# Router logits of a mixture-of-experts kernel in plain f32, with two weight splits moved ahead of the routing

## What is computed

```
def moe_swiglu(x, router_w, router_b, w_gate_up, w_down):
    B, S, D = x.shape                      # 1, 256, 1024
    xf = x.reshape(-1, D)
    logits = jnp.einsum('td,de->te', xf, router_w) + router_b     # 8 experts
    top_v, top_i = lax.top_k(logits, TOP_K)                       # TOP_K = 2
    gates = jax.nn.softmax(top_v, axis=-1)
    combine = jnp.sum(gates[..., None] * jax.nn.one_hot(top_i, N_EXPERTS), axis=1)
    for e in range(N_EXPERTS):
        y = y + combine[:, e:e + 1] * swiglu(xf, w_gate_up[e], w_down[e])
```

## Time and profile before

| what | us |
|---|---|
| median of 3 executions | 2058.91 |
| lowest and highest | 2049.66, 2062.65 |
| the profiled execution, its own time | 2062.65 |
| its span | 2060.9 |
| mean granted TensorE clock, share of full | 0.954 |

### The profile page before, as it was taken

How to read it: one execution, slowest core, us unless ns; L and a number is a source line. 1 busy time by engine, 2 the same in 40 slices (tenths; PEclk the granted TensorE clock), 3 DMA queues, 4 the chain that set the end, 5 groups by cost and what they waited for, 6 DMA issues and landing times.

```text
span 2060.9 us, 26596 instructions
## 1 busy us (share of the span) xinstructions
PE 1961.6 (95%) x10038; PEld 1608.1 (78%) x10051; DVE 1395.9 (68%) x1162; ACT 1129.9 (55%) x991; POOL 59.2 (3%) x81
## 2 busy tenths in 40 slices
PE   8978999999999998798999999999999999999987
PEld 6756998786789976686778778778787877888875
DVE  4444776444454545537888878888788888888875
ACT  5333554352243433514666767767676676776762
POOL 2230000100000000000000000000000000000000
PEclk8979999998899999778999999999999999999999
DMA  6604445442245545113999989999999999999980
GB/s 232 203 31 143 160 166 184 154 143 82 82 149 203 193 134 184 62 42 104 359 333 325 360 315 346 349 326 355 333 349 347 321 345 326 345 356 329 351 296 31
DMA packets 251591, 486.93 MB, mean 236 GB/s; under 512 B 14108, under 2 KB 19292, under 8 KB 251536
## 3 DMA queue, kind: packets, MB, share of 16 engines
q1 hardware_dynamic: 244976, 477.30, 65.9%
q0 software_dynamic: 6560, 8.91, 1.5%
HBM read 484.05 MB, written 1.05 MB: 235 GB/s over the span
## 4 chain that ended last, share of the span: by engine, by line
PE 59%; DMA 14%; DVE 13%; ACT 7%; issue 4%; DVEq 2%; SPq 0%; POOL 0%; ACTq 0%; POOLq 0%
DMA w_raw<-in_moe_w_down 8%; DVE w_lo L887 7%; PE psum L1908 7%; PE psum L1910 7%; PE psum L1909 7%; PE psum L1500 6%; PE psum L1502 6%; PE psum L1501 6%; ACT w_hi L521 6%; DMA w_raw<-in_moe_w_gate_up 6%; PE psum L1531 3%; PE psum L1533 3%; PE psum L1534 3%; PE psum L1551 2%; PE psum L1654 1%
## 5 line engine op out<-in xcount | busy, mean ns | idle before, releaser
L887 DVE TENSOR_TENSOR w_lo<-w_raw,w_hi 128x2048 fp32r<-128x2048 f32 (+2 forms) x475 | 1029.7, 2196 | 354.5 <-ACT w_hi L521 351.0
L521 ACT ACTIVATE w_hi<-w_raw 128x2048 fp32r<-128x2048 f32 (+2 forms) x475 | 862.3, 1838 | 273.4 <-DMA w_raw<-in_moe_w_gate_up 105.7
L1908 PE MATMUL psum<-w_hi,xg_hi 128*128 128x512 f32 x896 | 361.0, 403 | 0.8 <-DVE xg_lo L1333 0.4
L1909 PE MATMUL psum<-w_lo,xg_hi 128*128 128x512 f32 x896 | 355.1, 396 | 0.0
L1910 PE MATMUL psum<-w_hi,xg_lo 128*128 128x512 f32 x896 | 355.0, 396 | 0.0
L1531 PE MATMUL psum<-xt_hi,w_hi 128*128 128x256 f32 (+1 forms) x840 | 235.2, 280 | 2.5 <-DVE w_lo L887 1.9
L1533 PE MATMUL psum<-xt_lo,w_hi 128*128 128x256 f32 (+1 forms) x840 | 234.7, 279 | 0.0
L1534 PE MATMUL psum<-xt_hi,w_lo 128*128 128x256 f32 (+1 forms) x840 | 234.5, 279 | 0.0
L1908 PEld LDWEIGHTS psum<-w_hi,xg_hi 128*128 128x128 f32 x896 | 169.0, 189 | 41.4 <-DVE w_lo L887 2.5
L1910 PEld LDWEIGHTS psum<-w_hi,xg_lo 128*128 128x128 f32 x896 | 168.9, 189 | 41.0
L1909 PEld LDWEIGHTS psum<-w_lo,xg_hi 128*128 128x128 f32 x896 | 169.2, 189 | 37.9
(11 more groups left out here) (362 smaller groups left out, 2041.6 us busy)
## 6 DMA issues: line engine op xcount, KB each, us to landing
w_raw<-in_moe_w_gate_up SPq DMA_DIRECT2D x224, 1024.0 KB, 6.7
w_raw<-in_moe_w_down SPq DMA_DIRECT2D x96, 1024.0 KB, 7.0
w_raw<-in_w_up SPq DMA_DIRECT2D x22, 1024.0 KB, 5.6
w_raw<-in_ffn_w_gate_up SPq DMA_DIRECT2D x22, 1024.0 KB, 5.5
w_raw<-in_moe_w_down SPq DMA_DIRECT2D x32, 512.0 KB, 4.5
w_raw<-in_w_in SPq DMA_DIRECT2D x12, 1024.0 KB, 6.7
w_raw<-in_ab_w_in SPq DMA_DIRECT2D x12, 1024.0 KB, 5.2
w_raw<-in_w_down SPq DMA_DIRECT2D x10, 1024.0 KB, 6.3
```

Source lines behind the costliest of these rows:

```text
L521: return act.activation(o, i, func, **kw)
L887: TT(w_lo[:, k % RING, 0:n], w_raw[:, k % RING, 0:n], w_hi[:, k % RING, 0:n].bitcast(F32), ALU.subtract)\
L1908: mm(o, hi[:, q, :], wh, start=(q == first), stop=False)
L1909: mm(o, hi[:, q, :], wl, start=False, stop=False)
```

## The change

The logits are no longer computed from rounded router weights. `rw_hi`, `rw_lo` and `logit_rows` are gone, with the ACT and DVE operations that made them and the two turns of the logits. PE multiplies the two parts of the turned `x`, read as plain f32, with `rw` as it was loaded: the tokens' part is now the stationary side (128 columns) and the 8 columns of `rw` are the moving side, so that the result stands with tokens on the partitions. On DVE `split_p(1)` and `splits(0, 2, 0)` now stand ahead of the first use of the logits.

```diff
@@ -240,15 +240,13 @@
         (busy_first,) = layout(at_phase, ("busy_first", [P, NB], BF16))
         (sig, p_out) = layout(at_phase, ("sig", [P, 2, NT, NB], F32), ("p_out", [P, NT, D], F32))
 
-        (xn_hi, xn_lo, xg_hi, xg_lo, mh_hi, mh_lo, mg, mh, rw, rw_hi, rw_lo) = layout(
+        (xn_hi, xn_lo, xg_hi, xg_lo, mh_hi, mh_lo, mg, mh, rw) = layout(
             at_phase, ("xn_hi", [P, NT, D], F32R), ("xn_lo", [P, NT, D], F32R), ("xg_hi", [P, KD, P], F32R),
             ("xg_lo", [P, KD, P], F32R), ("mh_hi", [P, KE, P], F32R), ("mh_lo", [P, KE, P], F32R),
-            ("mg", [P, NB], F32), ("mh", [P, 2, NB], F32), ("rw", [P, KD, N_EXP], F32), ("rw_hi", [P, KD, N_EXP], F32R),
-            ("rw_lo", [P, KD, N_EXP], F32R))
+            ("mg", [P, NB], F32), ("mh", [P, 2, NB], F32), ("rw", [P, KD, N_EXP], F32))
         (ys_hi, ys_lo, sel, selt, gslot) = layout(
             at_xt, ("ys_hi", [P, D], F32R), ("ys_lo", [P, D], F32R), ("sel", [P, NT, P], F32R),
             ("selt", [P, SEQ], F32R), ("gslot", [P, 1], F32))
-        (logit_rows,) = layout(at_xt + 2 * nbytes([P, D]) + 2 * nbytes([P, SEQ]) + 32, ("logit_rows", [N_EXP, SEQ], F32))
 
         psum = ctx.enter_context(nc.psum_tensor("psum", [P, 8, NB], F32))
         acc = [[psum[:, 2 * s + t, :] for t in range(NT)] for s in range(2)]
@@ -851,12 +849,8 @@
                 take_item(i + 1, k, r)
 
             if "moe" in live:
-                act.wait_ge(S("rw_landed"), 16)
-                copy(rw_hi[:], rw[:]).then_inc(S("rw_hi_ready"), 1)
                 operand(9)
                 copy(xn_hi[:], x[:]).then_inc(S("xn_hi_ready"), 1)
-                act.wait_ge(S("logits"), 1)
-                copy(logit_rows[:], scr[0:N_EXP, 0, 0:SEQ]).then_inc(S("logit_rows_ready"), 1)
                 round_p(1)
                 rounds(0, 2, 0)
                 act.wait_ge(S("top_gap"), 1)
@@ -1383,8 +1377,6 @@
             idxf = route[:, 234:250].rearrange("p (t e) -> p t e", e=8)
 
             if "moe" in live:
-                dve.wait_ge(S("rw_hi_ready"), 1)
-                TT(rw_lo[:], rw[:], rw_hi[:].bitcast(F32), ALU.subtract).then_inc(S("rw_split"), 1)
                 operand(9)
                 dve.wait_ge(S("xn_hi_ready"), 1)
                 TT(xn_lo[:], x[:], xn_hi[:].bitcast(F32), ALU.subtract)
@@ -1393,9 +1385,11 @@
                 dve.sem_inc(S("y_added"), 2)
                 dve.memset(one8, 1.0)
                 dve.tensor_copy(eid8, slot_row[:, 0:N_EXP])
+                dve.wait_ge(S("logits"), 1)
                 dve.wait_ge(S("rb_landed"), 16)
-                dve.wait_ge(S("logits_turned"), 1)
-                TT(logits, scr[:, 0, SEQ:SEQ + NT * N_EXP].rearrange("p (t e) -> p t e", e=N_EXP),
+                split_p(1)
+                splits(0, 2, 0)
+                TT(logits, scr[:, 0, 0:NT * N_EXP].rearrange("p (t e) -> p t e", e=N_EXP),
                    rb_row[:].unsqueeze(1).broadcast_to([P, NT, N_EXP]), ALU.add)
                 dve.drain()
                 for t in range(NT):
@@ -1413,7 +1407,7 @@
                 dve.drain()
                 TT(selm, hot1, hot2, ALU.add)
                 dve.drain().then_inc(S("chosen"), 1)
-                split_p(1)
+
 
                 dve.wait_ge(S("top_exp"), 1)
                 dve.wait_ge(S("ranks"), 1)
@@ -1441,7 +1435,6 @@
                 select(0)
                 TS(route_i[:, 3:4], eidf[:, 3:4], float(N_EXP), None, ALU.add).then_inc(S("counted"), 1)
                 TT(over_before, over_before, over, ALU.subtract)
-                splits(0, 2, 0)
                 take_item(0)
                 splits(2, 4, 0)
                 dve.drain()
@@ -1956,19 +1949,14 @@
             cur_pe = route[:, 232:234]
             if "moe" in live:
                 operand(9, x)
-                pe.wait_ge(S("rw_split"), 1)
-                for k in range(KD):
-                    o = scr[0:N_EXP, 0, 0:SEQ]
-                    mm(o, rw_hi[:, k, :], xt_hi[:, k, :], start=(k == 0), stop=False)
-                    mm(o, rw_hi[:, k, :], xt_lo[:, k, :], start=False, stop=False)
-                    m = mm(o, rw_lo[:, k, :], xt_hi[:, k, :], start=False, stop=(k == KD - 1))
+                pe.wait_ge(S("rw_landed"), 16)
+                for t in range(NT):
+                    for k in range(KD):
+                        for q, part in enumerate((xt_hi, xt_lo)):
+                            m = mm(scr[:, 0, t * N_EXP:(t + 1) * N_EXP], part[:, k, t * P:(t + 1) * P].bitcast(F32), rw[:, k, :],
+                                   start=(k == 0 and q == 0), stop=(k == KD - 1 and q == 1))
                 m.then_inc(S("logits"), 1)
                 turn_p(1)
-                pe.wait_ge(S("logit_rows_ready"), 1)
-                for t in range(NT):
-                    m = pe.transpose(scr[:, 0, SEQ + t * N_EXP:SEQ + (t + 1) * N_EXP], logit_rows[:, t * P:(t + 1) * P],
-                                     ident[0:N_EXP, 0:N_EXP])
-                m.then_inc(S("logits_turned"), 1)
                 pe.wait_ge(S("chosen"), 1)
                 sm = lambda t: route[:, 80 + 8 * t:88 + 8 * t]
                 mm(scr[:, 1, 0:8], tri_excl[:], sm(0), start=True, stop=True)
```

## The result

| | before | after |
|---|---|---|
| median of 10 executions each, us | 2056.76 | 2068.43 |
| lowest, highest | 2046.66, 2069.76 | 2063.33, 2074.6 |
| ratio, 95% interval | | 1.0061 [1.0041, 1.0082] |
| profiled execution: time, span | 2062.65, 2060.9 | 2073.3, 2071.6 |
| first logit matmul to first gather matmul, us | 12.03 | 26.17 |

The changed kernel is slower by 0.61%, which is 12.5 us of 2056.76. The ratio and its interval are an estimate of their own and not the quotient of the two medians, which lie 11.7 us apart. The forecast was +13 us, 2072 us, with a range of 2061 to 2082.

The account below looks back on a forecast made before the run. The prediction took PE in the expert loop, with the router's serial stretch on the path ahead, to bound the kernel; step times summed to a 13.3 us gather shift, 2058.9 + 13 = 2072 us, range 2061 to 2082.

Parts of the forecast that it names:

- That this stretch is on the path and a shift of the gather goes through: Router ahead of the expert loop: whatever moves the gather's start moves everything behind it; shift 13.3 us.
- Price of a call, 0.22 and 0.43: Logits on PE: each of 32 plain f32 calls takes 0.22 us at full clock, 0.43 at half.
- the case of doubled price: Rival for the logits on PE: each call costs twice the price, by whatever cause; +27 us, 2086; chance 0.03.
- Clock falls 3.7 us behind the start: Logits on PE: 17 calls run at full clock, then 15 at half take 6.5 us; 10.2 us in all.
- The rival of the clock that holds: Logits on PE: the clock stays full through all calls; +9.8 us, 2069; chance 0.14.
- The sum, station by station: Router: step times from the first logit call at 942.05 to the gather at 967.45, a shift of 13.3 us.
- Removed operations cost nothing and give nothing: Router: dropping the logits' copy and two turns saves nothing; dropping rw_lo readies the operand about 0.15 us earlier.
- The moved splits lose their cover: DVE ahead of the logit add: ppt_lo and two w_lo (4.49 us a pair) now delay the routing, add at 960.3.
- The exp gives 0.6 back: ACT in the routing: the exp no longer comes last but well before the ranks end; 0.6 us gained.
- The loop takes up to 5.8 us back: Rival in the expert loop: if loads pace it, two early loads recover up to 5.8 us; +7.5, 2066; chance 0.10.
- Slower by over 1%: Clock at 0.50 well into the first expert, +21 to +25 us, or doubled call price; chance 0.12 together.
- The sign of being wrong: Gather to end: a distance changed by more than 2 us would speak against the prediction.

Follow-up runs that it names:

- the control: The changed kernel run once more with no edit: ratio 1.0053 [1.0026, 1.0079] to the kernel before.
- only the logits: The changed kernel with DVE's old order, so that split_p(1) and splits(0, 2, 0) stand behind the routing again: ratio 1.0052 [1.0028, 1.0077] to the kernel before.
- the hoisted splits: The changed kernel with ACT rounding and DVE splitting weight chunks 0 and 1 while PE computes the logits: ratio 1.0021 [1.0003, 1.0039] to the kernel before.
- the kernel with only the order: The kernel before with split_p(1) and splits(0, 2, 0) moved ahead of DVE's first use of the logits, logits unchanged: ratio 1.0029 [1.0006, 1.0052].

## Why the prediction was right

- *That this stretch is on the path and a shift of the gather goes through.* Right: 14.1 us at the gather, 14.1 at chunk 4, 12.5 [8.4, 16.9] by the ratio.
- *Price of a call, 0.22 and 0.43.* Right at both clocks, with two records per call. The Trainium skill's four passes (page "FP8 and Floating Point Precision", section "TensorE Precision Notes") did not make a call 0.44 at full clock; the measurement decides, and the case of doubled price is out.
- *Clock falls 3.7 us behind the start.* It fell after 3.0 and, in the control, 2.8 us; in the kernels with only the logits and with the hoisted splits after 2.4 and 3.1. The two delays of the rows, 2.6 and 3.3, enclose three of these four, and none reaches the 3.7: the choice past both was the error. So 14 calls ran fast and not 17, and the calls took 10.9 to 11.1 us where the sum had 10.2. This is the term that was mis-sized, by 0.7 to 0.9 us. The rival of the clock that holds is out, and the kernel with wide matmuls between the calls shows that it would have been worth at least 1.8 us: 9.1 instead of 10.9, with 15 matmuls more in it.
- *The sum, station by station.* Counted from the first call, which the sum had 0.15 earlier than before, its gather stands at +25.4 (967.45 - 942.05); measured 26.17. It was 0.8 behind at ppt_hi, 0.6 at the bias add and 0.8 again at the slots, because the sum let DVE go on as the ranks end (2.29), and 2.41 passed.
- *Removed operations cost nothing and give nothing.* This was not tried by itself. What the traces show is that in the changed kernels the add follows what it waits for directly (+11.08 behind a block of 10.90 in the one with hoisted splits), as the sum had it. Without rw_lo the first call follows the last transposes of x by 2.67 us (932.78 to 935.45) instead of 2.80 (939.41 to 942.21): 0.13, where the sum had 0.15. The 14.1 leaves this out, since it counts from the first call.
- *turn_p at half clock.* Estimated 0.9; ppt_hi follows the start of the four transposes by 1.13, against 0.64 at full clock.
- *The moved splits lose their cover.* Right, 5.5 us alone. In the sum this term stood inside the chain and had no number of its own; the kernel with only the order gives it one.
- *The exp gives 0.6 back.* Right in the changed kernel, where from ranks to slots 2.41 us pass instead of 2.92: DVE waits for L1966 and not for ACT. With DVE's old order the exp is the last again and costs 3.99 us of waiting.
- *The loop takes up to 5.8 us back.* Not seen in the traces as far as chunk 4, whose split has the full shift. The stretch from there to the end was 1086 and 1079 us for the kernel before and 1089 and 1077 for the changed one, which differ more between executions than between kernels, so a gain of a few us could hide in it. The two ratios of the changed kernel lie 1.6 and 3.5 us below the shift; the intervals hold both readings, and this stays open.
- *Slower by over 1%.* The clock came back at 976.0 in the first trace, 5.8 us after the first item began at 970.22. Before it took 5.8 us too: 0.69 over the microsecond from 968 is a return at 968.6, not at 968.4 as the prediction read it. Out.
- *The sign of being wrong.* A distance from gather to end that changed by more than 2 us was to speak against the prediction, and it did change, by 3.3. The sign was badly chosen: the kernel before moved by 7.2 against itself.

The total alone does not bear out the mechanism. Its interval of 8.4 to 16.9 us would also hold the +9.8 of a clock that does not fall; the trace is what tells them apart. The 2072 came from a median of three executions that lay 2.1 us above that of ten, and the match in the total owes something to the spread of the kernel, which is larger than the term that was mis-sized.

## What to carry to other kernels

Price a small serial stage inside its own trace, from its first instruction to the first that the big loop needs, since the ten executions of the kernel before lay 23 us apart, nearly twice the effect of the change. A line that is moved ahead of a wait in an engine's program keeps its duration but loses what hid it; put it beside the longer operation instead, as the hoisted splits show (7.8 us for three moved lines). Where PE waits between narrow operations, matmuls on constants can pay for themselves, but look first at which engine holds the next step: here the gather was 3.3 us shorter and chunk 4 only 2.6 earlier, because DVE's splits came in between, and the measured ratio was 1.0000 [0.9978, 1.0022].

## What the runs showed of the hardware

- PE was busy without a gap in 8-column calls with 128-column weights, and the granted clock fell from 1.00 to 0.50 all the same, 3.0 and 2.8 us after the first of them, which follows the last wide matmuls directly. Fifteen 512-column matmuls among the calls kept it at 1.00, and the block became 1.8 us shorter by them.
- A 128x512 bf16 matmul between two f32 pairs added 0.14 us. In a row of their kind seven took 1.67 us and one by itself shows as 0.38, which makes a start every 0.22.
- A plain f32 call took 0.22 us with 128 weight columns and 8 moving ones, and 0.43 with 8 weight columns and 256 moving ones, both at full clock. Sixteen of the latter in a row left the clock at 1.00.
- The stretch ahead of the logits can differ between executions of one kernel: with the wide matmuls they began at 934.82 in one and 941.15 in another trace of the same program. The cause was not looked into.
